# Both feed-forward input stages: from activations moving to weights moving, and the product turned by VectorE and GpSimd

## The chip, the cores and the metric

One core of a Trainium2 chip. The time is device microseconds of one execution, the median over the runs; lower is better.

## What is computed

The reference is one block of a network on 256 tokens of width 1024 (a feed-forward part, a token mixer of retention and neighbourhood attention, a second feed-forward part) and then two recurrent or convolutional mixers. All in float32. The change touches only the two feed-forward parts, whose inner width is 2816:

```python
def _swiglu(x, w_in, w_out):
    g, u = jnp.split(x @ w_in, 2, axis=-1)
    return (jax.nn.silu(g) * u) @ w_out

# in the block, once at the start and once at the end:
h = _swiglu(_rms_norm(x, ffn1_pre_norm[l]), ffn1_w_in[l], ffn1_w_out[l])
x = x + 0.5 * _rms_norm(h, ffn1_post_norm[l])
```

## The kernel before, in words

**Operands.** A float32 product is made of three products of the float32r type: each operand is split into a rounded part ("hi") and the rest ("lo"), and hi x hi, hi x lo and lo x hi are summed. Activations lie turned in `xT` (width over partitions, 256 tokens along), with hi and lo side by side.

**Weights.** All weights come as one stream of 150 groups of 128x2048 (1 MB). SyncE loads them into a ring of six slots (`raw`, L414 to L418), waiting before each load for the event in `RELEASE` that says its slot is free. ScalarE rounds a group to `w_hi` (L522), VectorE subtracts to get `w_lo` (L996), TensorE waits for that (`lo_done`). ScalarE and VectorE do this in program order between their other work: `round_to(n)` and `low_to(n)` stand in the code where groups up to n are to be made. Each engine runs its own instructions strictly in the order written.

**A feed-forward input stage** has 22 groups, in two forms. Groups 0 to 3 are two column tiles (`column_tile`, L1710): the activations are the stationary operand, the weights move in pieces of 512 columns, 24 matmuls a group, and the result has tokens over partitions, 256 gate and 256 up columns. ScalarE takes silu of the gate columns (L645, L648), VectorE multiplies by the up columns (`up`, L1149) into `prod`, TensorE turns the 128x256 product by four transposes against the identity for each tile (`hidden_transposes`, L1821), and ScalarE and VectorE split it into `hT_hi` and `hT_lo`, the operand of the output stage. In the first part, silu takes the token factor of the norm as a scale for each partition.

Groups 4 to 21 are 18 chunks (`chunk`, L1827): the weights are stationary, the activations move. A chunk has two halves (gate, up) of eight pairs: `w_hi` with hi and lo tokens, 512 columns (L1839), and `w_lo` with hi tokens, 256 columns (L1841). The result has the width over partitions already and needs no turning; ScalarE and VectorE join the halves (L662 to L677, L1167 to L1188). Here the token factor of the first part lies along the free side, so VectorE makes two diagonal matrices and TensorE spreads them to a row (L1706).

**The output stage** (`out_stage`, L1769) goes over 11 groups of two chunks, 24 matmuls of 512 columns a group, in blocks of output groups (0, 1), 2, 3, 4, 5, 6 and (7 to 10), both token halves for each. `wait_chunk` waits for the hidden chunks.

**Banks.** `acc` has two banks for each token half t, used in turn by column tiles (`par`). TensorE may start tile j in a bank when `up` of tile j-2 has freed it.

**GpSimd** issues some loads (constants, gains, `bias_raw`), masks biases in the mixer and multiplies gates later; it has nothing to do in the feed-forward parts from 28 to 200 us.

Of the kernel before, what the change touches and what calls it, by code (L numbers as in the profile page):

```python
# [25 lines left out]
P = 128  # L26
S = 256
# [32 lines left out]
ACC_READERS = {"f1_in": "V" * 2, "f1_out": "V", "mix_in": "AVVVVVVVVAAAA", "na_out": "V", "mix_out": "V",  # L60
               "f2_in": "V" * 2, "f2_out": "V", "a_in": "AA", "a_out": "V", "b_in": "V" * 2, "b_out": "V"}
ACC_ORDER = "".join(ACC_READERS.values())
FIRST_ACC = {}
for _name in ACC_READERS:
# [3 lines left out]
FILL_COUNTS = [("f1_in", 2), ("t1", 4), ("rq", 2), ("rk", 2), ("rs", 4), ("rp", 4),  # L68
               ("yret", 4), ("merged", 4), ("t2", 4), ("f2_in", 2), ("t3", 4),
# [3 lines left out]
SPLIT_COUNTS = [("f1_in", 2), ("t1", 4), ("yret", 4), ("merged", 4), ("t2", 4),  # L73
                ("f2_in", 2), ("t3", 4), ("gate", 6), ("t4", 4), ("b_in", 12)]
# [5 lines left out]
STRAIGHT, CHUNKS = 4, 18  # L80
CHUNKS_BEFORE = {"f1_in": 0, "f2_in": CHUNKS}
# [5 lines left out]
for _name, _n in STAGES:  # L87
    for _g in range(_n):
        if _name in CHUNKS_BEFORE and _g >= STRAIGHT:
            RELEASE.append(("chunk", CHUNKS_BEFORE[_name] + _g - STRAIGHT + 1))  # L90
        elif _name == "a_in" and _g >= A_STRAIGHT:
# [33 lines left out]
def build(nc, first_in, weights, x_turned_in, x_in, gain0_in, gains, rot_in, colmask_in, dist_in, decay_in, lam_in, bias_in, gate_w_in,  # L125
          gate_b_in, conv_a_in, conv_ab_in, conv_b_in, out):
    with ExitStack() as ctx:
# [67 lines left out]
        prod = at("prod", [P, 2, T, 256], F32, area + 47104)  # L195
        gate_c = at("gate_c", [P, 2, S], F32, area + 51200)
        prod_c = at("prod_c", [P, 2, S], F32, area + 53248)

        warm = at("warm", [P, P + 256], F32, area + 63488)
        rstd0_diag = at("rstd0_diag", [P, T, P], F32, area + 65536)  # L200
        rstd0_row = at("rstd0_row", [P, S], F32, area + 66560)
# [60 lines left out]
        rstd0_diag_ready = sem("rstd0_diag_ready")  # L262
        rstd0_row_full = sem("rstd0_row_full")
        rstd0_row_ready = sem("rstd0_row_ready")
# [9 lines left out]
        gate_chunk_full = sem("gate_chunk_full")  # L274
        chunk_full = sem("chunk_full")
        gate_part = sem("gate_part")
        up_part = sem("up_part")
        gate_summed = sem("gate_summed")
        up_summed = sem("up_summed")
        silu_ready = sem("silu_ready")  # L280
        prod_ready = sem("prod_ready")
        chunk_hi = sem("chunk_hi")
        chunk_lo = sem("chunk_lo")
# [99 lines left out]
        def _(sp):  # L383
# [30 lines left out]
            for g in range(RING, NG):  # L414
                kind, n = RELEASE[g - RING]
                sp.wait_ge({"used": group_used, "acc": acc_full[1], "acc0": acc_full[0], "ret": ret_acc_full, "pair": pair_full, "b_half": b_half_full,
                            "chunk": chunk_full}[kind], n)
# [13 lines left out]
        def _(pool):  # L431
# [29 lines left out]

            load_bias(0)
            load_bias(1)
            pool.wait_ge(bank_full, FIRST_FILL["t1"] + 4)
# [30 lines left out]
            load_gains(3, 5, 6)  # L495
            pool.wait_ge(x_ready, 2 * 2 + 1)
# [17 lines left out]
        def _(act):  # L514
# [69 lines left out]
            def opening():  # L584

                def token_sums(t):
                    act.wait_ge(x_landed[t], 16)
                    step(a.activation(prod[:].rearrange("p a t n -> p (a t n)"), x[:, t], ACT.Square,
# [43 lines left out]
            def swiglu(which, normed):  # L632

                st = f"{which}_in"
                g0, c0, f0 = FIRST_GROUP[st], FIRST_ACC[st], FIRST_FILL[st]
# [14 lines left out]
                def hidden_hi(j, par):  # L650
                    act.wait_ge(bank_full, f0 + 1 + j)
                    dst = hT_hi[:, bass.ds(2 * j, 2), :] if not isinstance(j, int) else hT_hi[:, 2 * j:2 * j + 2, :]
                    a.activation(dst, aux[:, par].rearrange("p (c q) -> p c q", c=2), ACT.Copy).then_inc(bank_hi, 1)

                c_before = CHUNKS_BEFORE[st]

                def gate_second_part(n):

                    act.wait_ge(gate_chunk_full, c_before + n + 1)
                    if n >= 2:  # L660
                        act.wait_ge(chunk_lo, c_before + n - 1)
                    a.activation(gate_c[:, n % 2], acc[:, n % 2, 0, S:2 * S], ACT.Copy).then_inc(gate_part, 1)  # L662

                def up_second_part(n):

                    act.wait_ge(chunk_full, c_before + n + 1)
                    a.activation(prod_c[:, n % 2], acc[:, n % 2, 1, S:2 * S], ACT.Copy).then_inc(up_part, 1)

                def chunk_silu(n):

                    act.wait_ge(gate_summed, c_before + n + 1)
                    a.activation(gate_c[:, n % 2], gate_c[:, n % 2], ACT.Silu).then_inc(silu_ready, 1)

                def chunk_round(n):

                    act.wait_ge(prod_ready, c_before + n + 1)
                    a.activation(hT_hi[:, STRAIGHT + n, :], prod_c[:, n % 2], ACT.Copy).then_inc(chunk_hi, 1)  # L677
# [13 lines left out]
                hidden_hi(0, 0)  # L691
                if g0 == 0:
# [5 lines left out]
                for n in range(CHUNKS):  # L698
# [4 lines left out]
                    if n == 0:  # L703
                        hidden_hi(1, 1)
# [283 lines left out]
        def _(dve):  # L988
# [150 lines left out]
            def swiglu(which):  # L1139
# [64 lines left out]
                if g0 == 0:  # L1204
                    rates()
# [1018 lines left out]
```

## Time and profile before

| | us |
|---|---|
| Median of the runs (889.08 to 890.57) | 889.22 |
| Span of the profiled execution | 887.0 |
| TensorE busy | 879.6 (99%) |
| VectorE busy | 625.0 (70%) |
| ScalarE busy | 489.4 (55%) |
| GpSimd busy | 64.4 (7%) |
| Weights loads: 147 of 1 MB | 4.8 from issue to landing (median) |

A profile is one execution. Its span runs from the first to the last instruction, and the time of a run is somewhat longer. Matmuls are pipelined: what a matmul costs in a stream is the distance between starts, not its own duration. "Idle before" with a releaser names who ended a wait. DMA share is the mean busy share of the core's 16 DMA engines.

### The profile page before, as it was taken

Reading aid. Unit: us, or ns where it says so; the run is one execution under the profiler, and the core shown is the slowest. Engines: PE = TensorE matmul, PEld = TensorE weight load, DVE = VectorE, ACT = ScalarE, POOL = GpSimd, SP = SyncE. Lnnn points to the kernel's source line nnn. Section 1 sums busy time; section 2 is a strip of 40 time slices with the busy share of each in tenths; the row PEclk is TensorE's granted clock in tenths of the full one; section 3 lists DMA queues with packets and bytes.
Section 4 is the critical chain, followed back from the end, with each engine's and each line's share of the span. In section 5 each row is a group of like instructions: output and inputs, shape, how many; then the busy total and the mean of one; then the engine's idle time right before and its main releaser. Section 6 shows DMA issues by size and latency. Waiting matters only on the chain.

```text
span 887.0 us, 11473 instructions
## 1 busy us (share of the span) xinstructions
PE 879.6 (99%) x4628; PEld 752.3 (85%) x4628; DVE 625.0 (70%) x808; ACT 489.4 (55%) x661; POOL 64.4 (7%) x89
## 2 busy tenths in 40 slices
PE   9999999999999999999999999999999999999997
PEld 7888888888888888888888888888999888888886
DVE  6887776467767656577577777446979857888872
ACT  6865564445444556446565555435887644555551
POOL 2000000003021110000000000000390000000000
PEclk9999999999999999999999999999999999999999
DMA  9955555455753444455655555546534456555521
GB/s 352 368 188 191 191 189 199 147 190 179 282 198 127 180 168 173 184 190 190 237 190 190 191 190 190 189 182 251 184 106 181 151 187 254 190 190 191 190 95 48
DMA packets 26948, 169.89 MB, mean 192 GB/s; under 512 B 3616, under 2 KB 3664, under 8 KB 7952
## 3 DMA queue, kind: packets, MB, share of 16 engines
q1 hardware_dynamic: 24368, 161.23, 50.3%
q0 software_dynamic: 2240, 7.66, 2.5%
q8 instruction: 37, 0.61, 0.3%
q10 hardware_dynamic: 288, 0.27, 0.1%
q14 instruction: 15, 0.12, 0.0%
HBM read 167.05 MB, written 1.05 MB: 190 GB/s over the span
## 4 chain that ended last, share of the span: by engine, by line
PE 97%; DVE 1%; ACT 1%; issue 0%; ACTq 0%
PE acc L1839 15%; PE acc L1642 15%; PE acc L1640 15%; PE acc L1641 15%; PE acc L2101 8%; PE acc L1841 7%; PE acc L2103 4%; PE acc L1655 2%; PE acc L1883 2%; PE acc L2053 2%; PE acc L2054 2%; PE acc L2052 2%; PE aux L2037 1%; PE aux L1764 1%; PE acc L1885 1%; PE aux L1641 1%
## 5 line engine op out<-in xcount | busy, mean ns | idle before, releaser
L996 DVE TENSOR_TENSOR w_lo<-raw,w_hi 128x2048 fp32r<-128x2048 f32 x147 | 336.8, 2300 | 89.9 <-ACT w_hi L522 89.5
L522 ACT ACTIVATE w_hi<-raw 128x2048 fp32r<-128x2048 f32 x145 | 275.7, 1911 | 62.6 <-DMA raw<-weights 62.4
L1839 PE MATMUL acc<-xT,w_hi 128*128 128x512 f32 x576 | 200.4, 394 | 0.0
L1841 PE MATMUL acc<-xT,w_lo 128*128 128x256 f32 x576 | 159.7, 277 | 0.0
L1839 PEld LDWEIGHTS acc<-xT,w_hi 128*128 128x128 f32 x576 | 108.0, 188 | 25.0
L1640 PE MATMUL acc<-w_hi,xT 128*128 128x512 f32 x312 | 124.0, 398 | 0.0
L1642 PE MATMUL acc<-w_hi,xT 128*128 128x512 f32 x312 | 121.8, 390 | 0.0
L1641 PE MATMUL acc<-w_lo,xT 128*128 128x512 f32 x312 | 121.5, 390 | 0.0
L2101 PE MATMUL acc<-xT,w_hi 128*128 128x512 f32 x320 | 111.3, 394 | 0.0
L1841 PEld LDWEIGHTS acc<-xT,w_lo 128*128 128x128 f32 x576 | 108.2, 188 | 0.0
L2103 PE MATMUL acc<-xT,w_lo 128*128 128x256 f32 x320 | 88.7, 277 | 0.0
L2101 PEld LDWEIGHTS acc<-xT,w_hi 128*128 128x128 f32 x320 | 60.0, 188 | 13.8
L1642 PEld LDWEIGHTS acc<-w_hi,xT 128*128 128x128 f32 x312 | 58.6, 188 | 12.6
L1640 PE MATMUL acc<-w_hi,hT_hi 128*128 128x512 f32 x176 | 68.7, 390 | 0.0
L1640 PEld LDWEIGHTS acc<-w_hi,xT 128*128 128x128 f32 x312 | 58.6, 188 | 11.8 <-issue 0.6
L1642 PE MATMUL acc<-w_hi,hT_lo 128*128 128x512 f32 x176 | 68.5, 389 | 0.0
L1641 PE MATMUL acc<-w_lo,hT_hi 128*128 128x512 f32 x176 | 68.5, 389 | 0.0
L1641 PEld LDWEIGHTS acc<-w_lo,xT 128*128 128x128 f32 x312 | 58.7, 188 | 11.4
L2103 PEld LDWEIGHTS acc<-xT,w_lo 128*128 128x128 f32 x320 | 60.1, 188 | 0.0
L677 ACT ACTIVATE hT_hi<-prod_c 128x256 fp32r<-128x256 f32 x36 | 15.1, 418 | 43.4 <-DVE prod_c L1182 43.4
L1640 PEld LDWEIGHTS acc<-w_hi,hT_hi 128*128 128x128 f32 x176 | 33.0, 188 | 6.9
L1641 PEld LDWEIGHTS acc<-w_lo,hT_hi 128*128 128x128 f32 x176 | 33.0, 188 | 6.8
(263 smaller groups left out, 1290.4 us busy)
## 6 DMA issues: line engine op xcount, KB each, us to landing
raw<-weights SPq DMA_DIRECT2D x147, 1024.0 KB, 4.8
gain_pre<-gains POOLq DMA_DIRECT2D x5, 512.0 KB, 5.0
raw<-weights SPq DMA_DIRECT2D x4, 512.0 KB, 7.5
gain_post<-gains POOLq DMA_DIRECT2D x3, 512.0 KB, 5.6
gate_w<-gate_w_in POOLq DMA_DIRECT2D x1, 1536.0 KB, 8.5
x_turned<-x_turned_in SPq DMA_DIRECT2D x4, 256.0 KB, 4.9
x<-x_in SPq DMA_DIRECT2D x2, 512.0 KB, 11.6
bias_raw<-bias_in POOLq DMA_DIRECT2D x16, 64.0 KB, 3.2
```

The source lines that it names most:

```text
L522: a.activation(w_hi[:, g % RING], raw[:, g % RING], ACT.Copy).then_inc(hi_done, 1)
L996: v.tensor_tensor(w_lo[:, slot], raw[:, slot], w_hi[:, slot].bitcast(F32), ALU.subtract)\
L1640: m.matmul(dst, hi[:, k, cols], w_hi[:, slot, w], start=first, stop=False)
L1641: m.matmul(dst, hi[:, k, cols], w_lo[:, slot, w], start=False, stop=False)
L1642: return m.matmul(dst, lo[:, k, cols], w_hi[:, slot, w], start=False, stop=last)
L1655: i = m.matmul(acc[:, t, column], xT[:, k, t * P:(t + 1) * P], w[:, g, unit * UNIT:(unit + 1) * UNIT], start=k == 0 and xT is xT_hi and w ...
L1839: m.matmul(dst, w_hi[:, slot, w], xT[:, k].rearrange("p a q -> p (a q)"), start=k == 0, stop=False)
L1841: i = m.matmul(dst[:, 0:S], w_lo[:, slot, w], xT[:, k, 0], start=False, stop=k == KD - 1)
L1883: m.matmul(dst, w_hi[:, g % RING, w], xT[:, k].rearrange("p a q -> p (a q)"), start=k == 0, stop=False)
L2052: m.matmul(dst, w_hi[:, slot, w], xT_hi[:, k, :], start=k == 0, stop=False)
L2101: m.matmul(dst, w_hi[:, g % RING, w], xT[:, k].rearrange("p a q -> p (a q)"), start=k == 0, stop=False)
L2103: i = m.matmul(dst[:, 0:S], w_lo[:, g % RING, w], xT[:, k, 0], start=False, stop=k == KD - 1)
```

## The change

All 22 groups of a feed-forward input stage become column tiles: 11 tiles of two groups, weights moving. The stream's order of weights follows (the two lines in `_stream` that differ are left out below). Chunks, their readers on ScalarE and VectorE, the token factors along the free side and the transposes of products on TensorE go. The product of a tile is turned in two steps: VectorE's transpose of the 128x512 product turns each 32x32 block in place in its quarter of 32 partitions (`turned`), and GpSimd's DMAs carry the blocks to the right quarter of partitions (`hT_raw`, which lies where `hT_lo` is made). One DMA carries from one quarter to one quarter the blocks of two tiles: 32 partitions with 8 runs of 128 B each; 16 DMAs for a turn of two tiles (half the runs for the last, single tile), 96 for a stage. `turned` has two buffers. ScalarE rounds tiles j-4 and j-3 behind the weights of tile j (j = 4, 6, 8, 10), the last three inside the output stage.

```diff
+TILES = 11
+TURNS = (TILES + 1) // 2
+QUADS = P // 32
+MOVES = QUADS * QUADS
...
-        if _name in CHUNKS_BEFORE and _g >= STRAIGHT:
-            RELEASE.append(("chunk", CHUNKS_BEFORE[_name] + _g - STRAIGHT + 1))
...
+            def move_tiles(before):
+
+                for p in range(TURNS):
+                    chunks = 4 * p, min(4 * p + 4, FF // P)
+                    n = chunks[1] - chunks[0]
+                    pool.wait_ge(tile_turned, before + chunks[1] // 2)
+                    for i in range(QUADS):
+                        for q in range(QUADS):
+                            quad = slice(32 * q, 32 * q + 32)
+                            pool.dma_start(hT_raw[quad, chunks[0]:chunks[1], :, i, :].rearrange("p c t b -> p (c t) b"),
+                                           turned[32 * i:32 * i + 32, p % 2, 0:n, :, q, :]
+                                           .rearrange("p c t b -> p (c t) b")).then_inc(tiles_moved[p % 2], 16)
...
             load_bias(0)
             load_bias(1)
+            move_tiles(0)
...
             load_gains(3, 5, 6)
+            move_tiles(TILES)
...
+                def hidden_hi(j):
+
+                    p = j // 2
+                    act.wait_ge(tiles_moved[p % 2], 16 * MOVES * (before // TILES * TURNS // 2 + p // 2 + 1))
+                    a.activation(hT_hi[:, 2 * j:2 * j + 2, :], hT_raw[:, 2 * j:2 * j + 2].rearrange("p c t i b -> p c (t i b)"),
+                                 ACT.Copy).then_inc(tile_hi, 1)
...
+                for j in range(2, TILES):
+                    silu(j, j % 2, 0)
+                    round_to(g0 + 2 * j + 5)
+                    silu(j, j % 2, 1)
+                    round_to(g0 + 2 * j + 6)
...
+                    if j >= 4 and j % 2 == 0:
+                        hidden_hi(j - 4)
+                        hidden_hi(j - 3)
...
+                round_to(g1 + 5)
+                hidden_hi(TILES - 3)
+                hidden_hi(TILES - 2)
+                round_to(g1 + 7)
+                hidden_hi(TILES - 1)
...
+                def turn_tile(j):
+
+                    p = j // 2
+                    for t in range(T):
+                        dve.wait_ge(acc_free_dve[t], prods0 + 1 + j)
+                    if p >= 2 and j % 2 == 0:
+                        dve.wait_ge(tiles_moved[p % 2], 16 * MOVES * (before // TILES * TURNS // 2 + p // 2))
+                    v.transpose(turned[:, p % 2, j % 2 * 2:j % 2 * 2 + 2].rearrange("p c t q b -> p (c t q b)"),
+                                prod[:, j % 2].rearrange("p c t n -> p (c t n)")).then_inc(tile_turned, 1)
...
-                    if t == 0:
-                        pe.wait_ge(rstd0_diag_ready, T)
-                        for k in range(T):
-                            i = m.matmul(aux[:, 2, k * P:(k + 1) * P], warm[:, 0:P], rstd0_diag[:, k],
-                                         start=True, stop=True)
...
-                hidden_transposes(0, 0)
-                for c in range(CHUNKS):
-                    chunk(c)
-                    if c == 0:
-                        hidden_transposes(1, 1)
...
+                for j in range(2, TILES):
+                    for t in range(T):
+                        pe.wait_ge(acc_free_dve[t], prods0 + j - 1)
+                        column_tile(g0 + 2 * j, j % 2, t)
```

VectorE's order at the start of the first stage, before; `prod` is a tile's product, `w_lo` the low part of a weight group (groups 4 and 5 here), `ls` small tables for the mixer:

```order
L1149 TENSOR_TENSOR prod<-acc,silu_g 128x256
L996 TENSOR_TENSOR w_lo<-raw,w_hi 128x2048
L1149 TENSOR_TENSOR prod<-acc,silu_g 128x256 x2
L996 TENSOR_TENSOR w_lo<-raw,w_hi 128x2048
L1149 TENSOR_TENSOR prod<-acc,silu_g 128x256
L1155 TENSOR_TENSOR hT_lo<-aux,hT_hi 128x512
L1122 TENSOR_SCALAR ls_67<-logit 128x20
```

The same place now:

```order
L1128 TENSOR_TENSOR prod<-acc,silu_g 128x2x128
L979 TENSOR_TENSOR w_lo<-raw,w_hi 128x2048
L1128 TENSOR_TENSOR prod<-acc,silu_g 128x2x128
L1139 STREAM_TRANSPOSE turned<-prod 128x512
L1128 TENSOR_TENSOR prod<-acc,silu_g 128x2x128
L979 TENSOR_TENSOR w_lo<-raw,w_hi 128x2048
```

The turning of tile 0 now stands ahead of the low part of group 5, and the small tables have moved behind tiles 3 and 5.

TensorE behind the second column tile of the first stage, before (the first row is the tile's last matmul):

```order
L1642 MATMUL acc<-w_hi,xT 128x512
L1821 MATMUL aux<-ident,prod 128x128 x4
L1839 MATMUL acc<-xT,w_hi 128x512
L1841 MATMUL acc<-xT,w_lo 128x256
L1839 MATMUL acc<-xT,w_hi 128x512
```

and now, where the first row is again the last matmul of that tile:

```order
L1612 MATMUL acc<-w_hi,xT 128x512
L1610 MATMUL acc<-w_hi,xT 128x512
L1611 MATMUL acc<-w_lo,xT 128x512
L1612 MATMUL acc<-w_hi,xT 128x512
L1610 MATMUL acc<-w_hi,xT 128x512
```

The transposes are gone, and tile 2 follows with three matmuls of 512 columns where two pairs stood. On GpSimd the moves stand between the first two bias loads and the load of `dist` (80 DMAs of 32x8x32 elements and 16 of 32x4x32), and in the second part between the gains and `gate_w`.

## Rows read from the trace of the kernel before

**Rows 1.** Page: busy time of each engine; chain that ended last, by engine and line.
```profile
PE 879.6 (99%) x4628; PEld 752.3 (85%) x4628; DVE 625.0 (70%) x808; ACT 489.4 (55%) x661; POOL 64.4 (7%) x89
PE 97%; DVE 1%; ACT 1%; issue 0%; ACTq 0%
```

**Rows 2.** Table by stage: us, busy of PE, PEld, DVE, ACT, POOL; PEclk, DMA share, GB/s.
```profile
29.05:129.52 100.47, 100.47 (x584) 87.89 (x582) 80.62 (x129) 63.74 (x96) 0.00 (x0) 1.00 0.59 214
129.52:190.29 60.77, 60.77 (x274) 50.38 (x273) 32.37 (x24) 27.09 (x23) 0.00 (x0) 1.00 0.52 186
...
437.40:537.87 100.47, 100.47 (x584) 87.88 (x582) 70.16 (x90) 61.74 (x92) 0.00 (x0) 1.00 0.55 194
```

**Rows 3.** Timeline of TensorE, first stage: start, us, line, what.
```profile
25.51 0.60 PE L1706 MATMUL aux<-rstd_diag,warm 128*128 128x128 f32 x4
25.88 0.48 PE L1640 MATMUL acc<-w_hi,xT 128*128 128x512 f32 x1
26.19 0.40 PE L1641 MATMUL acc<-w_lo,xT 128*128 128x512 f32 x1
...
28.70 0.60 PE L1821 MATMUL aux<-ident,prod 128*128 128x128 f32 x4
29.05 0.48 PE L1839 MATMUL acc<-xT,w_hi 128*128 128x512 f32 x1
...
129.52 0.39 PE L1640 MATMUL acc<-w_hi,hT_hi 128*128 128x512 f32 x1
```

**Rows 4.** Timeline of TensorE, second stage: its transposes, and the first output matmul.
```profile
437.04 0.60 PE L1821 MATMUL aux<-ident,prod 128*128 128x128 f32 x4
...
537.87 0.39 PE L1640 MATMUL acc<-w_hi,hT_hi 128*128 128x512 f32 x1
```

**Rows 5.** Timeline of TensorE, end of the first output stage.
```profile
188.03 1.03 PE L1764 MATMUL aux<-ident,tmp 128*128 128x128 f32 x8
188.82 0.48 PE L1640 MATMUL acc<-w_hi,hT_hi 128*128 128x512 f32 x1
...
190.29 0.39 PE L1640 MATMUL acc<-w_hi,xT 128*128 128x512 f32 x1
```

**Rows 6.** Timeline of VectorE ahead of the first chunks.
```profile
27.91 0.75 DVE L1149 TENSOR_TENSOR prod<-acc,silu_g 128x256 f32<-128x256 f32 x2
28.58 2.29 DVE L996 TENSOR_TENSOR w_lo<-raw,w_hi 128x2048 fp32r<-128x2048 f32 x1
```

**Rows 7.** Groups: line, what, xcount; busy us, mean ns; idle before and its releaser.
```profile
L996 DVE TENSOR_TENSOR w_lo<-raw,w_hi 128x2048 fp32r<-128x2048 f32 x147 | 336.8, 2300 | 89.9 <-ACT w_hi L522 89.5
L522 ACT ACTIVATE w_hi<-raw 128x2048 fp32r<-128x2048 f32 x145 | 275.7, 1911 | 62.6 <-DMA raw<-weights 62.4
...
L532 ACT ACTIVATE xT<-aux 128x512 fp32r<-128x512 f32 x20 | 11.2, 597 | 32.7 <-PE aux L1987 18.2 <-PE aux L1764 14.3
L1024 DVE TENSOR_TENSOR xT<-aux,xT 128x512 fp32r<-128x512 f32 x16 | 10.5, 688 | 15.4 <-ACT xT L532 15.4
```

**Rows 8.** GpSimd: timeline rows of two issues, and the group of the bias loads.
```profile
17.45 0.71 POOL L450 DMA_DIRECT2D colmask<-colmask_in  x1 [15.96 <-DMA raw<-weights]
...
21.31 0.53 POOL L452 DMA_DIRECT2D logit<-lam_in  x1
...
L460 POOL DMA_DIRECT2D bias_raw<-bias_in x16 | 8.8, 551 | 4.1 <-POOL bias_m L477 4.1
```

**Rows 9.** DMA: queues and landings, of 17 to 30 us, 0 to 4 us, the page.
```profile
q1 hardware_dynamic: 752, 4.82, 92.8%
...
colmask<-colmask_in POOLq DMA_DIRECT2D x1, 48.0 KB, 5.4
logit<-lam_in POOLq DMA_DIRECT2D x1, 6.0 KB, 8.4
...
q10 hardware_dynamic: 144, 0.00, 2.0%
...
q0 software_dynamic: 2240, 7.66, 2.5%
```

More of the change, by code:

```diff
@@ L273, in build @@
         gate_ready = [sem(f"gate_ready{t}") for t in range(T)]
[L274 to L283, printed above, removed]
+        tile_turned = sem("tile_turned")
+        tiles_moved = [sem(f"tiles_moved{b}") for b in range(2)]
+        tile_hi = sem("tile_hi")
+        tile_lo = sem("tile_lo")
         bank_full = sem("bank_full")
@@ L1106, in opening @@
                     v.reciprocal(rstd0[:, t:t + 1], std[:, 2 + t:3 + t]).then_inc(rstd0_ready, 1)
-                dve.wait_ge(rstd0_ready, T)
-                for t in range(T):
-                    if t == 0:
-                        dve.wait_ge(ident_ready, 1)
-                    v.tensor_scalar(rstd0_diag[:, t], ident[:], rstd0[:, t:t + 1], None, ALU.mult)\
-                        .then_inc(rstd0_diag_ready, 1)
             v.memset(warm[:], 1.0).then_inc(warm_set, 1)
@@ L1141, in swiglu @@
                 st = f"{which}_in"
-                g0, f0, q0 = FIRST_GROUP[st], FIRST_FILL[st], FIRST_SPLIT[st]
+                g0, before = FIRST_GROUP[st], TILES_BEFORE[st]
+                prods0 = ACC_ORDER[:FIRST_ACC[st]].count("V")
                 gate0 = {"f1": 0, "f2": GATES_F2}[which]
@@ L1191, in swiglu, with hidden_lo @@
+                def hidden_lo(j):
+                    chunks = slice(2 * j, 2 * j + 2)
+                    dve.wait_ge(tile_hi, before + j + 1)
+                    v.tensor_tensor(hT_lo[:, chunks, :], hT_raw[:, chunks].rearrange("p c t i b -> p c (t i b)"),
+                                    hT_hi[:, chunks, :].bitcast(F32), ALU.subtract).then_inc(tile_lo, 1)
                 if g0 == 0:
@@ L1200, in swiglu @@
                     up(0, 0, 1)
+                    turn_tile(0)
                 low_to(g0 + 6)
                 up(1, 1, 1)
-                hidden_lo(0, 0)
-                if g0 == 0:
-                    rates()
-                for n in range(CHUNKS):
-                    chunk_gate(n)
-                    low_to(g0 + 7 + n)
-                    chunk_up(n)
-                    if n == 0:
-                        hidden_lo(1, 1)
-                    chunk_product(n)
-                    chunk_low(n)
-                low_to(g0 + 25)
-                low_to(FIRST_GROUP[f"{which}_out"] + GROUPS[f"{which}_out"])
-            GATES_F2 = 2 + 2
+                turn_tile(1)
+                low_to(g0 + 7)
+                for j in range(2, TILES):
+                    up(j, j % 2, 0)
+                    low_to(g0 + 2 * j + 5)
+                    up(j, j % 2, 1)
+                    turn_tile(j)
+                    low_to(g0 + 2 * j + 6)
+                    if j == 3 and g0 == 0:
+                        rates()
+                    if j == 5 and g0 == 0:
+                        log_rates()
+                    if j >= 4 and j % 2 == 0:
+                        hidden_lo(j - 4)
+                        hidden_lo(j - 3)
+                g1, n1 = FIRST_GROUP[f"{which}_out"], GROUPS[f"{which}_out"]
+                low_to(g1 + 5)
+                hidden_lo(TILES - 3)
+                hidden_lo(TILES - 2)
+                low_to(g1 + 7)
+                hidden_lo(TILES - 1)
+                low_to(g1 + n1)
+            GATES_MIX = TILES
+            GATES_F2 = GATES_MIX + 2
             swiglu("f1")
@@ L1808, in swiglu @@
                 st = f"{which}_in"
[L1809 to L1842 removed]
+                g0, before = FIRST_GROUP[st], TILES_BEFORE[st]
+                prods0 = ACC_ORDER[:FIRST_ACC[st]].count("V")
                 if n == 0:
```

158 lines of the change are left out of this document (28 added, 130 removed).

## The prediction

> **What bounds the kernel now.** First the page's busy times and its chain of waits: TensorE is busy 879.6 of 887.0 us and carries 97% of the chain that ended last [rows 1]. So the time falls only where TensorE gets less to do, and rises only where it is made to wait. Next the table by stage: in both feed-forward input stages TensorE is busy for the whole stretch, 100.47 of 100.47 us twice, and so in the output stage behind the first one [rows 2]. VectorE is busy 80.6 us of the first stretch and ScalarE 63.7, the DMA engines 0.59 of it; that is the cover that new work can use. The profiled execution has a span of 887.0 us against a median of 889.22 us over the runs shown: some 2.2 us lie around the span, and I carry them over unchanged.
>
> **The change part by part.**
>
> *TensorE, the products.* An old chunk group is 2 halves of 8 pairs, a pair being one matmul of 512 columns and one of 256: 32 matmuls, 12288 columns. A group of a new column tile is 24 matmuls of 512 columns: also 12288. The columns don't change; 8 matmuls fewer per group do. The first stage runs from the transposes at 28.70 to the first output matmul at 129.52, the second from 437.04 to 537.87: 100.82 and 100.83 us for 18 groups and two sets of transposes each [rows 3, 4]. The price of the new form is read in the output stage, which consists of it: 264 matmuls of 512 columns between 129.52 and 190.29, less 0.79 us for the eight transposes at 188.03, and 0.08 us by which the matmul behind such a group is spaced longer (25.88 to 26.19 is 0.31, where 0.23 is usual) [rows 3, 5]: (60.77 - 0.87) / 264 = 0.2269 us. The new stretch is 18 x 24 = 432 matmuls, 98.02 us. Gain: 2.80 + 2.81 = 5.61 us, of which 4 x (0.35 + 0.08) = 1.72 us are the four sets of transposes of the products, which leave TensorE altogether [rows 3], and 3.9 us come from 288 fewer matmuls, 13.5 ns each. This agrees with the columns: 512 columns at the 2.4 GHz of a full clock are 213.3 ns, and 226.9 were taken.
>
> The Trainium skill (TensorE: Matmul & The Clock Gate, "Wait — 56ns, not 53.3ns?") gives a fixed cost of about 2.5 ns per matmul at the full clock. By that page the 288 matmuls are worth 0.7 us instead of 3.9 and the forecast would be 886.9 us; the rows give 13.5 ns in both forms, and the sum goes by the rows.
>
> *TensorE, the row of factors.* Only the old chunk form needs the token factors along the free side, so the matmuls of rstd0_diag go: 25.51 to 25.88, 0.37 us, and 0.08 us on the matmul behind them [rows 3]. Gain 0.45 us.
>
> *VectorE's order at the start.* Here one wait appears. The weights' low part of group 5 starts at 28.58 and takes 2.29 us. Ahead of it stand, in the new order, the same two products (27.91, 0.75 us for both) and the turning of tile 0 [rows 6]. VectorE's transpose is not in the trace. From below it is bounded by a pass over half as many elements (0.42 us, the half of the two products, rounded up), from above by two passes over 128x512 (2 x 0.69); I take one such pass, 0.69 us, as the size is the same [rows 6, 7]. Low part done: 28.58 + 0.65 + 2.29 = 31.5 us. TensorE starts tile 2 0.80 us earlier than chunk 0 now starts (the factors' matmuls and the transposes ahead of chunk 0 are gone), at 28.25, and wants group 5 after 12 matmuls, at 28.25 + 2.72 = 31.0. Wait: 0.5 us, between 0.3 and 1.2. The old order wanted group 5 only one chunk later. In the second stage the same group is early, since its low part stands ahead of tile 2 by more than the turning costs; nothing is lost.
>
> *VectorE and ScalarE in the steady part.* A tile lasts 48 x 0.2269 = 10.9 us. VectorE does two products (0.75), one turn (0.69), two weights' low parts (4.6) and one hidden low part (0.69): 6.7 us. ScalarE does two roundings of weights (3.8) and three short passes; each has at most the elements of a 128x512 one and stays under 0.7 us, so under 6 us [rows 6, 7]. Old chunks kept VectorE busy 80.6 us a stage, nine new tiles 60 us; ScalarE's 63.7 fall likewise [rows 2]. So both get freer. A weight group's rounding stands behind the silu at a tile's end and is wanted 13.6 us later, which leaves 13.6 - 0.5 - 1.9 - 2.3 = 9 us. Silu's and Exp's tables are changed at tile 4 instead of ahead of the chunks; two loads on ScalarE lie inside that slack. Cost nothing, as long as the tiles' waits for the moves are short.
>
> *GpSimd's moves.* Per stage 96 transfers, in turns of 16, a turn being two tiles and due every 21.8 us. This is the one unknown. Three prices bound it. Issue: 0.53 to 0.55 us each now, with 128 rows described [rows 8]; a new one describes 256 pieces, so 0.53 if the time is fixed, 1.07 if it goes with the pieces: 8.5 to 17 us a turn, under 21.8 either way. Landing: of eight small transfers issued from 17.45 to 21.31, the first landed 5.4 us and the last 8.4 us after its issue, at 22.9 and 29.7, seven steps of 0.97 us, with the weights' queue holding the DMA engines at 0.93 [rows 8, 9]: they overlap, and at that pace a turn is 15.5 us. Engine time: a turn is 4096 pieces of 128 B, 256 for each engine. A tiny packet took 0.02 x 16 x 4 us / 144 = 9 ns; the mean packet of GpSimd's queue, at 3.4 KB, took 0.025 x 16 x 887 / 2240 = 158 ns [rows 9]. So 2.3 to 40 us a turn; I take about 13 ns, near the tiny packet since 128 B are nearer to it, hence 3.3 us beside 11.3 us for weights, in 21.8. All three fit: I cost the moves at nothing. What hides them is the distance: a tile is wanted by ScalarE three tiles, 33 us, after its turn was issued.
>
> **Sum.** 5.61 + 0.45 - 0.5 = 5.56 us; 887.0 - 5.6 = 881.4 span, 889.22 - 5.56 = **883.7 us**. With the straight form at 0.2275 us, as where transfers are dense, 0.5 us more; with no wait at the start, 0.5 us less.
>
> **Rivals.**
> *A. The moves follow one another.* If a move holds GpSimd's path until it has landed, its price is c, and the queue grows above 21.8 / 16 = 1.36 us. The first turn is ready at about 30.5 us; the last tile's rounding stands ahead of output group 7, which TensorE wants 38 us after the input stage's end at 126.8; less rounding and low part, all 96 moves must be down by 160.5. That is 130 us for 96: c = 1.35 us decides. At c = 2.0 each stage ends 192 - 130 = 62 us late: 883.7 + 124 = 1008 us, slower. At 1.5 it is 883.7 + 28 = 912. For it: even the first small transfer took 5.4 us to land, and the trace has no 96 in a row. Against it: the 0.97 us of [rows 9]. The Trainium skill (DMA: Bandwidth & Descriptors, "Anatomy of one DMA — SWDGE (gpsimd) path") puts about 2.0 us of fixed time on each such DMA; if that were paid in series it would be this rival, and the rows show it overlapped.
> *B. The moves are right but the weights come late.* A column tile gives its two ring slots back 2.7 us apart and then none for 8 us, where chunks gave one every 5.5; pieces of the moves also stand between weight packets. If this or a slow turning makes TensorE wait 1 to 2 us at the start of each stage, 885.5 to 887.7 us. Against it: the output stage has the same matmuls and a DMA share of 0.52, and TensorE never idles in it [rows 2].
> *C. The 13.5 ns per matmul don't belong to the count of matmuls but to the stage,* so that the new stretch is as long as the old without its transposes: 1.72 + 0.45 - 0.5 = 1.7 us, 887.5 us, hardly to be told from no change. Against it: both forms show the same 13.5 ns.
>
> **How the numbers follow.** A change under 0.2% (1.8 us) can't be told from none in this kernel. The forecast with its bounds (882.5 to 885.3) gets 0.72, A 0.12, B 0.11, C 0.05. The range reaches from the forecast's lower bound into B, 882.5 to 887.0: it leaves out A, C and a fifth of B. Faster by over 0.2% is below 887.4: forecast and most of B, 0.82; within 0.2%: C and the rest of B, 0.06; slower: A, 0.12.
>
> **What would show it.** Right: the first stage's product matmuls end near 127 us and start 0.227 us apart; one TensorE wait of about 0.5 us near 31 us, for the low part of the weights; GpSimd's issues under 1.1 us each, ended before the next turn; no wait of ScalarE for the moves; DMA share in the stages up by under 0.2. Wrong: VectorE's transpose waiting for moves at tile 4 or later; ScalarE's hidden rounding waiting for a DMA, with weight roundings queued behind it; TensorE waiting in the output stage; product matmuls 0.231 us apart.

## The result

The changed kernel takes **883.7 us** (median of 4 runs, 883.57 to 883.82) against 889.7 for the kernel before on the same chip (4 runs, 889.08 to 890.57): ratio 0.9932, 95% interval 0.9918 to 0.9946. In a second set it took 883.82 (5 rounds), ratio 0.9935 (0.9923 to 0.9948). The prediction was 883.7 and its range 882.5 to 887.0. It started from 889.22, the median of the three runs then shown; the fourth makes it 889.7, so the gain in this set is 6.0 us, and 5.5 in the second (889.29 to 883.82), where 5.56 was forecast. The profiled execution has a span of 882.0 us where it was 887.0, 5.0 less.

The page after, in the columns of [rows 1] and, for the DMA queue, of [rows 9]:

```profile
PE 873.6 (99%) x4320; PEld 737.3 (84%) x4320; DVE 602.2 (68%) x720; ACT 461.9 (52%) x570; POOL 174.5 (20%) x281
...
q0 software_dynamic: 8384, 13.44, 5.1%
...
L459 POOL DMA_DIRECT2D hT_raw<-turned x192 | 109.6, 579 | 122.0 <-DVE turned L1139 120.3
...
hT_raw<-turned POOLq DMA_DIRECT2D x160, 32.0 KB, 2.7
```

TensorE is busy 6.0 us less, with 308 matmuls fewer: 288 by the form of the groups, 16 transposes, 4 for the row of factors. VectorE and ScalarE are freer by 22.8 and 27.5 us. GpSimd has 110 us more, in which it does nothing but issue 192 moves of 0.58 us, and its queue's share of the DMA engines goes from 2.5 to 5.1%.

The stages after, in the columns of [rows 2]. The first row starts at tile 2, where the first chunk was; the third starts inside tile 1 of the second stage:

```profile
28.65:127.59 98.94, 98.38 (x433) 81.08 (x433) 67.51 (x76) 48.94 (x47) 45.53 (x80) 1.00 0.71 238
127.59:188.34 60.75, 60.75 (x274) 50.38 (x272) 32.21 (x26) 29.47 (x27) 9.26 (x17) 1.00 0.58 205
434.77:532.99 98.22, 98.22 (x435) 81.31 (x434) 60.93 (x52) 44.36 (x43) 45.65 (x80) 1.00 0.65 219
```

In the first stage TensorE is busy for 98.38 of 98.94 us; the 0.56 us are one recorded wait. In the output stage nothing changed, though moves still run in it. The DMA share of the first stage is 0.71 where it was 0.59, in the second 0.65 where it was 0.55: up by 0.12 and 0.10.

TensorE's timeline after (the columns of [rows 3]): the last matmul of tile 1 and tile 2 behind it, the first output matmul, then the first matmul behind the output stage, then the end of the second input stage:

```profile
28.34 0.39 PE L1612 MATMUL acc<-w_hi,xT 128*128 128x512 f32 x1
28.65 0.47 PE L1610 MATMUL acc<-w_hi,xT 128*128 128x512 f32 x1
28.96 0.39 PE L1611 MATMUL acc<-w_lo,xT 128*128 128x512 f32 x1
...
31.27 0.39 PE L1612 MATMUL acc<-w_hi,xT 128*128 128x512 f32 x1
32.22 0.50 PE L1610 MATMUL acc<-w_hi,xT 128*128 128x512 f32 x1 [0.56 <-DVE w_lo L979]
...
127.59 0.39 PE L1610 MATMUL acc<-w_hi,hT_hi 128*128 128x512 f32 x1
```

```profile
188.34 0.39 PE L1610 MATMUL acc<-w_hi,xT 128*128 128x512 f32 x1
```

```profile
532.76 0.39 PE L1612 MATMUL acc<-w_hi,xT 128*128 128x512 f32 x1
532.99 0.39 PE L1610 MATMUL acc<-w_hi,hT_hi 128*128 128x512 f32 x1
```

Against [rows 3 to 5] the start of the output stage came forward by 1.93 us (129.52 to 127.59), its end by 1.95 (190.29 to 188.34), and the start of the second output stage by 4.88 (537.87 to 532.99). So the first stage gave 1.93 and what lies from there to the second stage's end 2.95; behind it nothing more is gained but 0.1. The start of the products wanders from one profile to the next (22.79 before, 23.12 here, 22.87 in the second set, 22.5 to 23.6 over all eleven traces). Counted from it, the first stage's products take 104.47 us where they took 106.73: 2.26 us less (104.67 and 2.06 in the second set).

The wait is at 31.3 to 32.2: 0.95 us between two starts that are 0.227 apart elsewhere, 0.72 us lost. VectorE at that place shows why (start, us, line):

```profile
26.22 2.29 DVE L979 TENSOR_TENSOR w_lo<-raw,w_hi 128x2048 fp32r<-128x2048 f32 x1 [1.38 <-ACT w_hi L525]
28.43 0.42 DVE L1128 TENSOR_TENSOR prod<-acc,silu_g 128x256 f32<-128x256 f32 x1
28.95 0.71 DVE L1139 STREAM_TRANSPOSE turned<-prod 128x512 f32<-128x512 f32 x1
...
29.89 2.27 DVE L979 TENSOR_TENSOR w_lo<-raw,w_hi 128x2048 fp32r<-128x2048 f32 x1
```

The low part of group 5 starts at 29.89, behind the turn of tile 0 and a third product, and is done at 32.16; TensorE goes on at 32.22.

GpSimd's moves of the first stage (columns as before, x is the count of issues in one row):

```profile
33.61 9.25 POOL L459 DMA_DIRECT2D hT_raw<-turned  x16 [5.11 <-DVE turned L1139]
53.67 9.21 POOL L459 DMA_DIRECT2D hT_raw<-turned  x16 [10.82 <-DVE turned L1139]
75.44 9.21 POOL L459 DMA_DIRECT2D hT_raw<-turned  x16 [12.55 <-DVE turned L1139]
97.19 6.92 POOL L459 DMA_DIRECT2D hT_raw<-turned  x12 [12.55 <-DVE turned L1139]
104.70 2.31 POOL L459 DMA_DIRECT2D hT_raw<-turned  x4 [0.58 <-issue]
118.95 9.21 POOL L459 DMA_DIRECT2D hT_raw<-turned  x16 [11.95 <-DVE turned L1139]
129.82 8.69 POOL L459 DMA_DIRECT2D hT_raw<-turned  x16 [1.66 <-DVE turned L1139]
```

A turn of 16 moves is issued in 9.2 us, and the next is due 21.8 us behind it. Ahead of every turn GpSimd waits for VectorE's transpose, and for no landing. The single moves land 1.7 to 6.9 us behind their issue.

### The profile page after: what moved, and what is told of

Same layout as the page of the kernel before. It is cut to its first block, busy times and chain, and to the rows that moved or that the text cites. A ratio compares the mean times of both kernels' runs of the same rounds, so it can differ in the third digit from the quotient of the medians.

```text
span 882.0 us, 10831 instructions
## 1 busy us (share of the span) xinstructions
PE 873.6 (99%) x4320; PEld 737.3 (84%) x4320; DVE 602.2 (68%) x720; ACT 461.9 (52%) x570; POOL 174.5 (20%) x281
## 4 chain that ended last, share of the span: by engine, by line
PE 94%; DVE 2%; ACT 2%; DMA 1%; SPq 1%; issue 0%; ACTq 0%; DVEq 0%
PE acc L1610 22%; PE acc L1612 22%; PE acc L1611 22%; PE acc L2025 8%; PE acc L2027 4%; PE acc L1807 2%; PE acc L1977 2%; PE acc L1978 2%; PE acc L1976 2%; DMA raw<-weights 1%; DVE w_lo L979 1%; PE aux L1961 1%; PE aux L1728 1%; PE acc L1809 1%; PE aux L1611 1%; PE aux L1610 1%
## 5 line engine op out<-in xcount | busy, mean ns | idle before, releaser
L1610 PE MATMUL acc<-w_hi,xT 128*128 128x512 f32 x600 | 236.2, 394 | 0.6 <-DVE w_lo L979 0.6
L1612 PE MATMUL acc<-w_hi,xT 128*128 128x512 f32 x600 | 233.8, 390 | 0.0
L1611 PE MATMUL acc<-w_lo,xT 128*128 128x512 f32 x600 | 233.6, 389 | 0.0
L459 POOL DMA_DIRECT2D hT_raw<-turned x192 | 109.6, 579 | 122.0 <-DVE turned L1139 120.3
L1610 PEld LDWEIGHTS acc<-w_hi,xT 128*128 128x128 f32 x600 | 112.7, 188 | 24.4 <-DVE w_lo L979 1.0
L1612 PEld LDWEIGHTS acc<-w_hi,xT 128*128 128x128 f32 x600 | 112.6, 188 | 23.8
L1611 PEld LDWEIGHTS acc<-w_lo,xT 128*128 128x128 f32 x600 | 112.7, 188 | 22.6
L2025 PE MATMUL acc<-xT,w_hi 128*128 128x512 f32 x320 | 111.3, 394 | 0.0
L2027 PE MATMUL acc<-xT,w_lo 128*128 128x256 f32 x320 | 88.7, 277 | 0.0
L2025 PEld LDWEIGHTS acc<-xT,w_hi 128*128 128x128 f32 x320 | 60.0, 188 | 13.8
L2027 PEld LDWEIGHTS acc<-xT,w_lo 128*128 128x128 f32 x320 | 60.1, 188 | 0.0
L1128 DVE TENSOR_TENSOR prod<-acc,silu_g 128x256 f32<-128x256 f32 x44 | 18.6, 423 | 40.6 <-ACT silu_g L651 22.8
L1610 PE MATMUL acc<-w_hi,yT_hi 128*128 128x512 f32 x96 | 37.5, 390 | 0.0
```

The lines of the kernel that those rows point to most:

```text
L459: pool.dma_start(hT_raw[quad, chunks[0]:chunks[1], :, i, :].rearrange("p c t b -> p (c t) b"), turned[32 * i:32 * i + 32, p % 2, 0:n, :, q, :]
L1128: v.tensor_tensor(prod[:, par, :, t], acc[:, t, par, 256:512].rearrange("p (c n) -> p c n", c=2), silu_g[:, t].rearrange("p (c n) -> p c n ...
L1610: m.matmul(dst, hi[:, k, cols], w_hi[:, slot, w], start=first, stop=False)
L1611: m.matmul(dst, hi[:, k, cols], w_lo[:, slot, w], start=False, stop=False)
L1612: return m.matmul(dst, lo[:, k, cols], w_hi[:, slot, w], start=False, stop=last)
L2025: m.matmul(dst, w_hi[:, g % RING, w], xT[:, k].rearrange("p a q -> p (a q)"), start=k == 0, stop=False)
```

## The experiments

Theory: the gain is the fixed time of 288 matmuls (13.5 ns each), the four sets of transposes and the row of factors; one wait is paid for it, made by VectorE's order; the moves are hidden, since they overlap one another. Rivals: the 13.5 ns belong to the stage or are far smaller (rival C, and the price by the Trainium skill); the wait is not the order's; the moves cost something that the waits don't show (B), or cost only when they run one by one (A).

### Once more

The changed kernel, in five rounds.

> The changed kernel once more, on the chip of the other three, so that they can be set against it: 883.7 us, some 6 us under the kernel before.

Measured 883.82 us (882.88 to 884.3), before 889.29 (15 runs). The same wait stands in the trace, 0.56 us by its record, and from tile 2's first matmul to the first output matmul it is 98.94 us again. So the level and the wait are the kernel's.

### VectorE's order put back

```diff
                     up(0, 0, 1)
-                    turn_tile(0)
                     up(1, 1, 0)
...
                     up(0, 0, 1)
-                    turn_tile(0)
                 low_to(g0 + 6)
+                turn_tile(0)
                 up(1, 1, 1)
```

The turn of tile 0 goes behind the low part of the stage's group 5, in both stages; nothing else is moved.

> VectorE makes the low part of weight group 5 ahead of turning tile 0. Theory (the wait at the start of the first stage is the turning that stands ahead of that low part): the low part is done 0.7 us sooner, the 0.56 us of TensorE's wait near 32 us and the longer spacing around it go, 883.0 us, 0.6 to 0.7 under the changed kernel. Rival (the group is late because its load or its rounding is late): no change, 883.7 us, the wait stays and names ScalarE's rounding or a DMA behind it.

Measured 882.79 us (882.36 to 883.0), ratio to before 0.9924 (0.9911 to 0.9936): 1.0 us better than the changed kernel, where 0.6 to 0.7 was expected. Because the two intervals overlap, it ran again:

> The kernel with VectorE's low part of group 5 ahead of the turn of tile 0, once more, beside depth4 on the same chip. If its 1.0 us against the changed kernel is the order's own: 882.4 to 883.2 again, with no wait of TensorE for VectorE's low parts and a matmul each 0.227 us through the third tile of the products. If 1.0 us was partly chance of that chip: 883.0 to 883.4, the 0.6 to 0.7 us that the one wait is worth.

Measured 882.54 us (882.34 to 883.52), ratio 0.9926 (0.991 to 0.9943). Both times the gain is 1.0 us or a little over. VectorE's timeline in the first of the two:

```profile
28.11 0.75 DVE L1128 TENSOR_TENSOR prod<-acc,silu_g 128x256 f32<-128x256 f32 x2
28.77 2.28 DVE L979 TENSOR_TENSOR w_lo<-raw,w_hi 128x2048 fp32r<-128x2048 f32 x1
30.97 0.70 DVE L1139 STREAM_TRANSPOSE turned<-prod 128x512 f32<-128x512 f32 x1
```

and TensorE's, at the place where it had waited:

```profile
30.98 0.39 PE L1610 MATMUL acc<-w_lo,xT 128*128 128x512 f32 x1
31.20 0.39 PE L1611 MATMUL acc<-w_hi,xT 128*128 128x512 f32 x1
31.43 0.39 PE L1609 MATMUL acc<-w_hi,xT 128*128 128x512 f32 x1
...
126.63 0.39 PE L1609 MATMUL acc<-w_hi,hT_hi 128*128 128x512 f32 x1
```

Group 5's low part is done at 31.05, and no matmul is recorded as waiting for it. The wait was the order's. It also cost more than its own row says. Counted from the start of the products to the first output matmul, the two runs with the order put back take 103.36 and 103.66 us, and the changed kernel (twice), the one with fewer moves and the one of depth 4 (both below) take 104.39 to 104.67: 1.0 us in the mean, as the medians say. Of it 0.7 is the gap. The rest is wider spacing behind the gap (0.34 us for the first step, then 0.228 to 0.233 instead of 0.227 for ten) and what is lost at the start of tile 2.

That last part isn't the order's. In the changed kernel the ten steps of tile 2 ahead of the wait (28.96 to 31.27) are 0.231 us each, in the first run with the order put back (28.94 to 31.20) 0.226. But in its second run they are 0.231 as well (28.38 to 30.69), behind a late start of tile 2:

```profile
28.08 0.47 PE L1609 MATMUL acc<-w_hi,xT 128*128 128x512 f32 x1
28.38 0.39 PE L1610 MATMUL acc<-w_lo,xT 128*128 128x512 f32 x1
```

Its first step is 0.30 and the one before it 0.34, where 0.227 is usual. The low part of group 4, which tile 2 needs first, had ended at 27.93, just where TensorE wanted it (24 steps of 0.2267 from 22.52 end at 27.96). Over the traces the wide steps go with such a late start and not with the order. Where the step into tile 2 is 0.27 to 0.52 us (here, in the changed kernel in both sets, with fewer moves, at depth 4), the next is 0.30 to 0.31 and the ten behind it are 0.228 to 0.231 each. Where it is 0.22 to 0.23 (the first run with the order put back, and the split kernel and depths 1 and 2, which have the changed order), they are 0.226 to 0.227. Why matmuls behind a short stop stand a few nanoseconds further apart stays open.

### What a matmul costs by being one more

```diff
+                        if split_columns:
+                            for h in range(2):
+                                part = acc[:, t, par, h * S:(h + 1) * S]
+                                w = slice(unit * UNIT + h * S, unit * UNIT + (h + 1) * S)
...
+                                m.matmul(part, xT_hi[:, k, cols], w_lo[:, slot, w], start=False, stop=False)
...
-                        column_tile(g0 + 2 * j, j % 2, t)
+                        column_tile(g0 + 2 * j, j % 2, t, split_columns=n == 2)
```

In tiles 2 to 10 of the second stage each matmul of 512 columns is done as two of 256: the same columns in 432 more matmuls.

> In tiles 2 to 10 of the second stage each matmul of 512 columns is made as two of 256: 432 matmuls more, not a column more. Theory (each matmul costs some 13.5 ns beside its columns, so the gain of the changed kernel is its smaller count of matmuls): 432 x 13.4 ns = 5.8 us over the changed kernel, 889.5 us, and a spacing of 0.120 us. Rival by the Trainium skill (TensorE: Matmul & The Clock Gate, 'Wait — 56ns, not 53.3ns?'), 2.5 ns a matmul: 1.1 us over, 884.8 us, a spacing of 0.109. Second rival (the spacing belongs to the stage, not to the count): no change.

Measured 889.19 us (10 runs), ratio to before 0.9999 (0.999 to 1.0008): 5.4 us over the changed kernel in the same set, 12.4 ns for each added matmul. Between the first output matmuls of the two stages the traces have 411.12 us (126.71 to 537.83) instead of 405.40, 13.2 ns each. TensorE's timeline in the middle of it:

```profile
450.35 0.28 PE L1689 MATMUL acc<-w_hi,xT 128*128 128x256 f32 x1
450.47 0.28 PE L1690 MATMUL acc<-w_lo,xT 128*128 128x256 f32 x1
450.59 0.28 PE L1691 MATMUL acc<-w_hi,xT 128*128 128x256 f32 x1
```

Two of 0.120 us stand where one of 0.2267 stood, 13.3 ns more. The price belongs to the matmul and not to the stage: rival C falls. Each matmul here has a weight load of its own (4320 of each in the changed kernel, 4752 in this one), so the 13.3 ns are the price of the pair; no run tells how much of it is the load's. The Trainium skill (TensorE: Matmul & The Clock Gate, "Wait — 56ns, not 53.3ns?") gives about 2.5 ns for a matmul; by that page this kernel would have been 1.1 us slower than the changed one. The trace doesn't agree: it was 5.4.

### Fewer and larger moves

```diff
-MOVES = QUADS * QUADS
+MOVES = 1
...
+                    pool.dma_start(hT_raw[:, chunks[0]:chunks[1]].rearrange("p c t i b -> p (c t i b)"),
+                                   turned[:, p % 2, 0:n].rearrange("p c t q b -> p (c t q b)"))\
+                        .then_inc(tiles_moved[p % 2], 16)
```

> The 16 small moves of a turn become one DMA over 128 partitions, which carries nothing from quarter to quarter, so the hidden layer is wrong; the same bytes in 12 transfers instead of 192. Theory (the moves are hidden whole): no change, 883.7 us within 0.3, the wait near 32 us stays. Rival (small transfers slow the weights or TensorE a little): 0.5 to 2 us under the changed kernel.

The kernel leaves every block in its own quarter. Measured 883.31 us (883.1 to 883.62), ratio to before 0.9931 (0.9917 to 0.9944). With 12 transfers for 192 and GpSimd's queue at 4.0% of the DMA engines for 5.1, the median is 0.5 us lower, and the two intervals overlap; the wait of 0.56 us for group 5 is still there. So the cut into small transfers costs half a microsecond or nothing. What the bytes themselves cost isn't tested, since this kernel carries them too; the steps of 0.2267 us in the second stage leave little room for it.

### The form of the groups without VectorE's turning

```diff
+                def hidden_transposes(j):
...
+                    for c in range(2):
+                        for t in range(T):
+                            i = m.transpose(aux[:, j % 2, c * S + t * P:c * S + (t + 1) * P],
+                                            prod[:, j % 2, c, t], ident[:])
...
                 for j in range(2, TILES):
                     for t in range(T):
                         pe.wait_ge(acc_free_dve[t], prods0 + j - 1)
                         column_tile(g0 + 2 * j, j % 2, t)
+                        if t == 0:
+                            hidden_transposes(j - 1)
```

All tiles with weights moving, but TensorE turns the products as it did for tiles 0 and 1, 11 sets in each stage; the transposes of VectorE and the moves are gone.

> Weights moving in all 22 groups, but TensorE turns the products, 11 sets of four transposes a stage; no VectorE transpose and no moves. This is one half of the change alone. Theory (each set costs TensorE 0.43 us, the VectorE turn costs it only the wait at the start): 22 x 0.43 = 9.5 us more on TensorE than in the changed kernel, less the 0.7 us of the wait, 892.5 us, some 3 us slower than before; the turning by VectorE and GpSimd is what makes the form pay. Rival (the sets hide in part behind other work, or the form alone is the gain): 885 to 889 us.

Measured 893.56 us (893.37 to 893.8), ratio to before 1.0043 (1.0027 to 1.006): slower than the kernel before. Against the kernel with VectorE's order put back (882.8, which has no wait for group 5 either) 22 sets of transposes cost 10.8 us, 0.49 us each where 0.43 was read. The traces agree: from the start of the products to the first output matmul it is 108.16 us against 103.36, 0.48 for each of the ten sets in between. The first of them in the trace:

```profile
28.69 0.60 PE L1766 MATMUL aux<-ident,prod 128*128 128x128 f32 x4
29.05 0.48 PE L1593 MATMUL acc<-w_hi,xT 128*128 128x512 f32 x1
29.36 0.40 PE L1594 MATMUL acc<-w_lo,xT 128*128 128x512 f32 x1
```

So the 288 matmuls alone would not have paid: the 18 sets that come on top of the four of before cost 8.8 us, more than twice the 3.9 that they give. The change works because the turning leaves TensorE.

### How deep the moves must overlap

GpSimd waits ahead of a move until the one before it (depth 1), the second before it (depth 2) or the fourth before it (depth 4) has landed:

```diff
+                            done, m = before // TILES * TURNS // 2 + p // 2, QUADS * i + q
+                            if m >= 2:
+                                pool.wait_ge(tiles_moved[p % 2][m % 2], 16 * (MOVES // 2 * done + m // 2))
                             quad = slice(32 * q, 32 * q + 32)
...
-                                           .rearrange("p c t b -> p (c t) b")).then_inc(tiles_moved[p % 2], 16)
+                                           .rearrange("p c t b -> p (c t) b")).then_inc(tiles_moved[p % 2][m % 2], 16)
```

(as it stands for depth 2; the others differ in the number, and ScalarE and VectorE wait for all the semaphores of a turn.)

> GpSimd waits for each move to land before it issues the next. Theory (a move then costs issue and landing, about 2.7 us in all, and the stage is late by what 96 moves take over 130 us): 96 x 2.7 = 259, less 130, twice: 258 us over the changed kernel, some 1140 us; TensorE waits in the output stages, VectorE's turning and ScalarE's hidden rounding wait for moves from tile 4 on. Rival (the distance in the ring and in the turns hides more than reckoned, as the last moves of a stage are wanted late): under 1050 us.

Measured 1125.53 us (one run): 241.7 over the changed kernel. The waits of TensorE, ScalarE and VectorE for the moves or what stands behind them (us in total, times, longest):

```profile
PE acc L1613 <- DVE w_lo L982: 215.6, 13, 27.3
```

```profile
ACT hT_hi L660 <- DMA hT_raw<-turned: 319.6, 12, 35.2
```

```profile
DVE turned L1142 <- DMA hT_raw<-turned: 198.7, 8, 30.3
```

TensorE never waits for a move itself. ScalarE and VectorE do, and their weight roundings and low parts are queued behind. TensorE's waits are 215.6 us, and it is busy 899.8 us instead of 873.6 for the same instructions, 26 more, together 241.8. The second part is the clock: the page's row of it shows 5 to 9 tenths where the waits lie and 9 or more elsewhere, and from 127 to 277 us the granted clock was 0.76 in the mean.

```profile
PEclk9998779657899999999998886876599999999999
```

GpSimd's timeline has two kinds of moves:

```profile
33.09 0.61 POOL L462 DMA_DIRECT2D hT_raw<-turned  x1 [5.20 <-DVE turned L1142]
40.23 0.60 POOL L462 DMA_DIRECT2D hT_raw<-turned  x1 [6.54 <-DMA hT_raw<-turned]
...
47.84 0.58 POOL L462 DMA_DIRECT2D hT_raw<-turned  x1 [1.54 <-DMA hT_raw<-turned]
49.95 0.58 POOL L462 DMA_DIRECT2D hT_raw<-turned  x1 [1.52 <-DMA hT_raw<-turned]
```

Some are 2.1 us from issue to issue (0.58 and a wait of 1.5), others up to 7.1. The 96 of the first stage ran from 33.1 to 279.3, the landing of the last: 2.56 us each.

> GpSimd lets two moves be in flight. Theory with the threshold of 1.35 us a move: two in 2.7 us is 1.35 us each, just at the threshold, so 0 to 10 us over the changed kernel, 883.7 to 894 us, with ScalarE's or VectorE's waits for moves visible though TensorE hardly waits. Rival (the threshold lies much lower, the queue must be deep): over 910 us.

Measured 936.23 us (934.73 to 938.58), ratio 1.0526 (1.0505 to 1.0547). This expectation failed: 52.5 us over, where at most 10 was expected. I had taken it that two in flight overlap in every part of the stage. GpSimd's timeline at the start of the first stage and its last row there:

```profile
33.57 1.20 POOL L462 DMA_DIRECT2D hT_raw<-turned  x2 [5.24 <-DVE turned L1144]
40.71 1.16 POOL L462 DMA_DIRECT2D hT_raw<-turned  x2 [5.93 <-DMA hT_raw<-turned]
46.30 1.16 POOL L462 DMA_DIRECT2D hT_raw<-turned  x2 [4.43 <-DMA hT_raw<-turned]
```

```profile
182.46 1.19 POOL L462 DMA_DIRECT2D hT_raw<-turned  x2 [0.76 <-DMA hT_raw<-turned]
```

The first pairs are 7.1 and 5.6 us apart, the last 1.9. The table of windows (columns of [rows 2]) has for these two pairs, and for the last 13 us:

```profile
33.60:40.70 7.10, 7.10 (x33) 5.86 (x32) 5.44 (x4) 4.11 (x4) 1.17 (x2) 1.00 0.90 334
40.70:46.30 5.60, 5.60 (x26) 4.66 (x25) 4.56 (x4) 2.44 (x3) 1.16 (x2) 1.00 0.78 300
...
170.80:183.60 12.80, 7.93 (x23) 6.38 (x24) 5.78 (x4) 4.20 (x4) 7.67 (x14) 0.59 0.07 16
```

The slow pairs lie where the weights' loads hold the DMA engines at 0.8 to 0.9, the fast ones where the share is 0.07. From 33.6 to 184 the 96 moves took 1.57 us each. TensorE's waits and busy time account for the 52.5 us again:

```profile
PE acc L1615 <- DVE w_lo L983: 41.7, 6, 17.7
```

with 884.3 us busy, 10.7 more. The threshold of the prediction, 96 moves within 130 us, put 1.57 us at 2 x 96 x (1.57 - 1.35) = 42 us, and 2.56 at 232. The waits are 41.7 and 215.6, in near halves over the two stages (19.4 and 22.3, 108.2 and 107.5).

> GpSimd issues a move only when the fourth one before it has landed (four semaphores in place of one); otherwise the changed kernel. With one move in flight the first stage's 96 moves took 33.1 to about 279 us, 2.55 us each, with two 1.57 us each; the time was 241.7 and 52.5 us over the changed kernel's, where the threshold's sum of the prediction, 2 x 96 x (c - 1.35), gives 230 and 42. Theory (what counts is only the mean pace of the moves against 1.35 us each, and the pace comes from how many overlap): with four in flight c lies at about 0.8 to 1.0 us (half of 1.57, and more where a landing takes up to 6.9 us beside the weights), below 1.35, so nothing waits on TensorE: 883.7 to 884.3, with ScalarE's wait for the moves back at around a microsecond at most. Rival (long single landings beside the weights' loads, not the mean, held the kernel with two in flight; each such stall goes through to TensorE): 885 to 895, with waits of VectorE or ScalarE for moves of over 5 us each, and TensorE behind them.

Measured 883.68 us (883.07 to 884.15), ratio 0.9935 (0.992 to 0.995): the changed kernel's time. Its waits:

```profile
PE acc L1615 <- DVE w_lo L983: 0.6, 1, 0.6
```

```profile
ACT hT_hi L661 <- DMA hT_raw<-turned: 15.8, 4, 7.0
```

The theory had the time right and the waits wrong, the rival the reverse. ScalarE waits 15.8 us for moves, up to 7.0 in one piece, and TensorE only its 0.6 us for group 5. GpSimd waits 63.0 us for landings, and the first stage's last move is issued by 146.5, 1.18 us each from 33.6. In the changed kernel, with no limit, the same 96 are issued in 1.09 us each, and there VectorE's turns set the pace: GpSimd waits for them alone. Two in flight lie above 1.35 us and cost 52.5, four lie below and cost nothing that can be told. So the mean pace over the stage decides, and landings that held ScalarE up to 7.0 us were taken up by the three tiles' distance.

## Why the prediction was right, and where not

**The bound.** The mechanism was right: TensorE is 99% busy as before, and what was gained is work that it no longer has. Its busy time fell by 6.0 us and the span by 5.0; the difference is idle time: 0.56 us are the wait for group 5, and 0.5 one for a rounded weight group ahead of the products, which the trace of before doesn't have.

**The exact hit is luck.** By the sum the span was to be 881.4, and it was 882.0: the gain in the trace is 5.0 us, not 5.56. The time came out at 883.7 even so, since the forecast added 2.2 us around the span. That was the distance between one execution's span and the median of other runs. In each run for which both are known, the time is only 1.7 to 1.95 us over its own span (883.76 over 882.0 here). Nor is the measured gain in the medians known to better than half a microsecond: 6.0 and 5.5 in two sets, with runs of the kernel before from 888.4 to 890.8. The range was held with room to spare; the last digit means nothing.

**The products, 5.61 us.** Of the first stage's 98.94 us, 0.72 are the gap; 98.22 for 432 matmuls is 0.2274 each where 0.2269 was taken, 0.2 us. In the second the spacing is 0.2267. The 13.5 ns were 13.3 by spacing, 13.2 by the split kernel's trace. From the first stage's end to the second's 2.95 us were gained where 2.81 stood. The Trainium skill's 2.5 ns (TensorE: Matmul & The Clock Gate, "Wait — 56ns, not 53.3ns?") would have put the time at 886.9; the trace doesn't agree.

**The row of factors, 0.45 us, and the wait, 0.5.** In the first stage 2.80 + 0.45 - 0.5 = 2.75 us were forecast from the start of the products and 2.26 came. The missing 0.5 is the wait, the one term that was mis-sized. The stretch of 104.47 us is 1.1 us longer than its 456 matmuls at 0.2267 us each: 0.72 for the gap, some 0.3 for wider steps on both sides of it, 0.1 for a late start of tile 2. The prediction's working for the wait took group 5's low part to start at 28.58 + 0.65 = 29.2; it started at 29.89. Of these 0.66 us, 0.52 come from group 4's low part ahead of it, which ended at 28.51 instead of 27.99, and 0.14 from the short idle times between products and turn. The first is no effect of the order: group 4's low part starts at 25.37 to 26.22 in the eleven traces, at 25.37 in that of the split kernel, which has the changed kernel's order in this stage. TensorE too stands 0.4 us later at tile 2 (28.65 for 28.25), 0.33 because its products began later (23.12 for 22.79) and 0.1 because it waits for that part. How much the gap costs wanders with these starts: 0.42 and 0.46 us at depths 2 and 1, 0.53 in the split kernel, 0.72 to 0.75 in the other four traces with this order. By the two runs with the order put back the wait and what goes with it are worth 1.0 us, inside the bounds of 0.3 to 1.2 and twice the value taken.

**VectorE's transpose**, taken as 0.69 us, takes 0.71 (22 of them, 711 ns in the median). The choice among rows by size was right.

**GpSimd's moves, nothing.** An issue takes 0.58 us (bounds 0.53 and 1.07): 256 pieces cost hardly more to describe than 128 rows. A turn needs 9.2 us of 21.8. ScalarE waits for moves once, 0.4 us, in the output stage, where no wait was forecast, and it delays nobody. The twelve-transfer kernel puts the cutting into small ones at half a microsecond or nothing. VectorE's nine tiles, taken as 60 us, were 60.9 in the second stage and 67.5 in the first, whose stretch holds 24 more instructions; beyond the one wait they didn't hold TensorE up.

**Rival A** didn't come about here, but its mechanism is real once the queue is limited, and its threshold holds from both sides. What was wrong in its price is that it counted waits alone: TensorE's busy time grew by 26 and 11 us besides, in and behind the waits, where the granted clock fell. Its window was also placed loosely: the first turn starts at 33.6, not 30.5, since the turn of tile 1 had to be waited for. **Rival B** wanted a wait of 1 to 2 us at the start of each stage, by late weights or slow turning. One of 0.72 us came, in the first stage, by the turning's place in the order; in the second stage none. **Rival C** fell with the split kernel.

## What to carry to other kernels

Where TensorE is the bound and transposes of intermediates are on it, VectorE's block transpose and small DMAs between quarters of partitions take them off at no price that shows in the medians beyond half a microsecond, if the consumer stands a few tiles behind and enough moves are in flight: work out the mean time allowed for one (here 1.35 us) and measure the pace beside the weights' loads, not on a quiet queue. Fewer and longer matmuls pay 13 ns each (with the weight load of each), which is worth having only if the new form brings no transposes back. Any instruction put into VectorE's order at the start of a stage is to be held against the low part that TensorE wants next; moving one turn behind one low part here gives the best kernel of all, 882.5 to 882.8 us.

## What the runs showed that was not expected

- A matmul's fixed price, its weight load included, is the same for 256 and for 512 columns, 13.3 ns at the full clock (0.120 and 0.2267 us apart).
- Behind a short stop matmuls stand up to 0.233 us apart for some ten steps, 0.2267 elsewhere. This goes with the stop and not with VectorE's order. The cause stays open.
- A pair of moves takes 5.6 to 7.1 us where weights are loaded and 1.9 where they aren't, a single one 7.1 and 2.1: in both places two in flight halve the price of one, but the busy queue is three times as dear.
- Waits of up to 27 us on TensorE cost a further 12 to 26% of their length in a lower clock (26.2 us on 215.6, 10.7 on 41.7).
